# Row stages of a two-block network: the first 128 tokens' factor and turn apart, squares behind the rounded parts, the norm's sums and spreading 7 or 8 blocks later

## The reference

```python
def rmsnorm(x, g):
    xf = x.astype(jnp.float32)
    y = xf * lax.rsqrt(jnp.mean(xf * xf, axis=-1, keepdims=True) + EPS) * g.astype(jnp.float32)
    return y.astype(x.dtype)
...
        mixed = jnp.concatenate([rmsnorm(out_a, g_a), rmsnorm(out_b, g_b), rmsnorm(out_c, g_c)], axis=-1)
        x = x + rmsnorm(mixed @ w_out[l], attn_post_norm[l])

        h = rmsnorm(x, ffn_pre_norm[l])
        u = causal_depthwise_conv(h @ w_up[l], conv_w[l], conv_b[l])
        gate, up = jnp.split(u, 2, axis=-1)
        y = (jax.nn.gelu(gate, approximate=True) * up) @ w_down[l]
        x = x + rmsnorm(y, ffn_post_norm[l])
...
        h = modulate(rms_norm(x, norm_gains[layer, 0]), shift_m, scale_m)
        j = layer // 2
        if layer % 2 == 0:
            y = attn_hybrid_mixer(h, att_w_qkv[j], att_w_o[j], pos)
```

## Time and profile before

| what | value |
|---|---|
| median of 3 runs | 1041.67 us (1041.29 to 1041.73) |
| the profiled execution | 1041.22 us, its span 1039.4 us |
| TensorE matmul busy | 1020.3 us, 98% of the span |
| VectorE busy | 812.4 us, 78% |
| ScalarE busy | 594.4 us, 57% |
| GpSimd busy | 162.5 us, 16% |

### The profile page before, as it was taken

The page is one execution under the profiler, slowest core; times in us unless marked ns, Lnnn a source line. Parts: engine busy times, 40 slices in busy tenths (PEclk is TensorE's granted clock), DMA queues, the critical chain, the costliest instruction groups (busy, mean ns, idle before and its releaser), DMA issues.

```text
span 1039.4 us, 18373 instructions
## 1 busy us (share of the span) xinstructions
PE 1020.3 (98%) x7424; PEld 953.2 (92%) x7424; DVE 812.4 (78%) x1397; ACT 594.4 (57%) x1029; POOL 162.5 (16%) x167
## 2 busy tenths in 40 slices
PE   8999999999999999999999999999999999999997
PEld 8888898999889997999999889988999899999887
DVE  5778799999997977588999798885668676674553
ACT  6688676666446766665444455544465566544443
POOL 0000134333102100032212011201100123111010
PEclk9999999999999999999999999999999999999999
DMA  9833356777893433457998787553434536774441
GB/s 359 312 117 123 122 196 245 289 277 255 344 398 144 154 128 117 193 191 271 381 370 308 282 319 279 203 182 142 162 123 170 195 131 234 278 270 152 168 167 41
DMA packets 34609, 228.49 MB, mean 220 GB/s; under 512 B 3803, under 2 KB 4075, under 8 KB 10972
## 3 DMA queue, kind: packets, MB, share of 16 engines
q1 hardware_dynamic: 33884, 224.69, 57.8%
q0 software_dynamic: 640, 2.62, 0.6%
HBM read 224.68 MB, written 2.62 MB: 219 GB/s over the span
## 4 chain that ended last, share of the span: by engine, by line
PE 84%; DVE 9%; ACT 3%; DMA 2%; issue 1%; POOL 0%; POOLq 0%; SPq 0%; DVEq 0%; ACTq 0%
PE psum L1523 16%; PE psum L1524 15%; PE psum L1525 15%; PE psum L1567 9%; PE psum L1568 5%; DVE w_lo L2300 3%; PE psum L1592 2%; PE psum L1595 2%; PE psum L1594 2%; PE psum L1964 2%; PE psum L1966 2%; PE psum L1965 2%; DMA raw<-in_w_in 2%; ACT w_hi L825 1%; PE psum L1755 1%; DVE arena L2632 1%
## 5 line engine op out<-in xcount | busy, mean ns | idle before, releaser
L2300 DVE TENSOR_TENSOR w_lo<-raw,w_hi 128x1024 fp32r<-128x1024 f32 (+2 forms) x340 | 387.2, 1160 | 134.9 <-ACT w_hi L825 129.4
L825 ACT ACTIVATE w_hi<-raw 128x1024 fp32r<-128x1024 f32 (+2 forms) x340 | 334.3, 997 | 215.7 <-PE psum L1525 84.6
L1523 PE MATMUL psum<-h_hi,w_hi 128*128 128x256 f32 (+1 forms) x1128 | 319.6, 283 | 5.4 <-DVE w_lo L2300 3.1
L1524 PE MATMUL psum<-h_hi,w_lo 128*128 128x256 f32 (+1 forms) x1128 | 316.7, 281 | 0.0
L1525 PE MATMUL psum<-h_lo,w_hi 128*128 128x256 f32 (+1 forms) x1128 | 316.4, 280 | 0.0
L1523 PEld LDWEIGHTS psum<-h_hi,w_hi 128*128 128x128 f32 x1128 | 212.4, 188 | 8.6 <-DVE w_lo L2300 5.2
L1525 PEld LDWEIGHTS psum<-h_lo,w_hi 128*128 128x128 f32 x1128 | 212.3, 188 | 0.0
L1524 PEld LDWEIGHTS psum<-h_hi,w_lo 128*128 128x128 f32 x1128 | 211.6, 188 | 0.7 <-issue 0.7
L1523 PE MATMUL psum<-hid,w_hi 128*128 128x256 f32 (+1 forms) x532 | 152.8, 287 | 0.5 <-DVE w_lo L2300 0.4
L1525 PE MATMUL psum<-hid,w_hi 128*128 128x256 f32 (+1 forms) x532 | 150.0, 282 | 0.0
L1524 PE MATMUL psum<-hid,w_lo 128*128 128x256 f32 (+1 forms) x532 | 150.0, 282 | 0.0
(11 more groups left out here) (316 smaller groups left out, 1386.9 us busy)
## 6 DMA issues: line engine op xcount, KB each, us to landing
arena<-in_ada SPq DMA_DIRECT2D x48, 1024.0 KB, 6.9
raw<-in_gu SPq DMA_DIRECT2D x44, 1024.0 KB, 6.8
raw<-in_ret_in SPq DMA_DIRECT2D x24, 1024.0 KB, 4.8
raw<-in_up SPq DMA_DIRECT2D x22, 1024.0 KB, 4.8
raw<-in_dn SPq DMA_DIRECT2D x32, 704.0 KB, 4.2
raw<-in_qkv SPq DMA_DIRECT2D x12, 1024.0 KB, 5.0
raw<-in_down SPq DMA_DIRECT2D x11, 1024.0 KB, 8.4
raw<-in_ret_o SPq DMA_DIRECT2D x8, 1024.0 KB, 4.8
```

The source lines that it names most:

```text
L825: nc.scalar.activation(w_hi[chunk % SPLIT_SLOTS][:, a:b], raw[chunk % RAW_SLOTS][:, a:b], ACT.Copy)\
L1523: nc.tensor.matmul(out, w[0], hc, start=start, stop=False, skip_group_check=True)
L1524: nc.tensor.matmul(out, w[1], hc, start=False, stop=False, skip_group_check=True)
L2300: tt(w_lo[s][:, a:b], raw[chunk % RAW_SLOTS][:, a:b], w_hi[s][:, a:b].bitcast(F32), ALU.subtract)\
```

## The change

- The mean, the root and the factor are made for each token group r by itself. The means of group 0 follow the first two pieces (`row_mean`, `row_rstd` on VectorE, `row_roots` on ScalarE). Group 0's diagonal is made by ScalarE (`first_diag`), group 1's by VectorE. The factor is written with other constants (1.5 and -0.5 in place of -3 and -0.5), with the same number of operations.
- TensorE turns the eight tiles of group 0 first and then the eight of group 1. The banks of the turned tiles are laid out anew; VectorE is told after tiles 0, 2, 4, 6 and 7 of group 1 (`TURN_ENDS`), and tile 7 waits for the first addition to x, since it reuses tile 0's bank. The 18 filling matmuls become 14 in stage 0, and 4 between the groups in stage 1.
- `rows_by_gains` squares tile 0 after rounding tile 1, then tile 1 after 2, 2 after 4, 3 after 5, and tiles 4 to 7 after 7.
- The sums stand in front of block 9 of chunk 1 and the spreading in front of block 15.

```diff
             def turned_rows(k):
-            return (tra + att)[k // 2][:, k % 2 * S:k % 2 * S + S]
+            bank, at = ((tra[0], 0), (tra[1], 0), (tra[1], S), (att[0], 0), (att[0], S), (att[1], 0), (att[1], S), (tra[0], S))[k]
+            return bank[:, at:at + S]
+
+        TURN_ENDS = (0, 2, 4, 6, 7)
...
+            def row_roots(stage, r):
+                act.wait_ge(row_ms, 2 * stage + r + 1)
+                nc.scalar.activation(row_stat[:, 6 + r:7 + r], row_stat[:, r:r + 1], ACT.Sqrt).then_inc(row_root, 1)
+
+            def first_diag(stage):
+                act.wait_ge(row_factor, stage + 1)
+                nc.scalar.activation(row_diag_of(0), ident[:, :], ACT.Identity, scale=row_stat[:, 24:25]).then_inc(row_diag, 1)
...
                 for r in range(2):
+                    if r:
+                        row_roots(stage, 0)
                     for n in range(2):
                         if r == 1 and n == 1:
+                            first_diag(stage)
                             act.wait_ge(half_done, 2 * (ph.chunk0 + ph.n))
...
             def rows_by_gains(i):
+                squares = {1: (0,), 2: (1,), 4: (2,), 5: (3,), 7: (4, 5, 6, 7)}
                 for k in range(DT):
...
-                    square(i, k)
+                    for n in squares.get(k, ()):
+                        square(i, n)
...
             def turn_rows(ph, i):
                 stage = ROW_STAGE[i]
-                keep_busy(18, att[1])
...
+                if stage == 0:
+                    keep_busy(14, att[1])
+                else:
+                    pe.wait_ge(row_copied, 2)
+                pe.wait_ge(row_diag, 2 * stage + 1)
+                for k in range(DT):
+                    turn(k, 0)
+                if stage:
+                    keep_busy(4, sco[0])
                 units_done(pe, ph.unit0 + ph.units)
                 if stage == 0:
                     pe.wait_ge(row_y, 2)
...
+                pe.wait_ge(row_diag, 2 * stage + 2)
                 for k in range(DT):
...
+                    if k == DT - 1:
+                        pe.wait_ge(row_x, DT * stage + 1)
+                    ins = turn(k, 1)
+                    if k in TURN_ENDS:
                         ins.then_inc(row_turned, 1)
...
-            swiglu_phase("up", FFNPRE, 1, 8)
+            swiglu_phase("up", FFNPRE, 9, 15)
...
-            deferred_phase("qkv", L0, 1, spread_at=8)
+            deferred_phase("qkv", L0, 9, spread_at=15)
...
+            def row_mean(stage, r):
+                dve.wait_ge(row_sq, 4 * stage + 2 * (r + 1))
+                stt(row_stat[:, r:r + 1], row_stat[:, 28 + r:29 + r], EPS, row_stat[:, 30 + r:31 + r], ALU.add, ALU.add).then_inc(row_ms, 1)
+
+            def row_rstd(stage, r):
+                m, s, a, f = (row_stat[:, at + r:at + r + 1] for at in (0, 12, 18, 24))
+                dve.wait_ge(row_root, 2 * stage + r + 1)
+                link(nc.vector.reciprocal(s, row_stat[:, 6 + r:7 + r]))
+                link(stt(a, s, -0.5, m, ALU.mult, ALU.mult))
+                link(tt(a, a, s, ALU.mult))
+                ins = stt(f, a, 1.5, s, ALU.add, ALU.mult)
...
             def row_copies(ph, i):
                 for r, n in ((0, 0), (0, 1), (1, 0)):
+                    if r:
+                        row_mean(ROW_STAGE[i], 0)
+                        row_rstd(ROW_STAGE[i], 0)
...
-                dve.wait_ge(row_sq, 4 * (stage + 1))
-                stt(row_stat[:, 0:2], row_stat[:, 28:30], EPS, row_stat[:, 30:32], ALU.add, ALU.add).then_inc(row_ms, 1)
-                refine(row_root, stage + 1, row_stat, 2)
-                for r in range(2):
-                    ts(row_diag_of(r), ident[:, :], row_stat[:, 24 + r:25 + r], -0.5, ALU.mult, ALU.mult).then_inc(row_diag, 1)
+                if stage == 0:
+                    row_rstd(0, 0)
+                row_mean(stage, 1)
+                row_rstd(stage, 1)
+                ts(row_diag_of(1), ident[:, :], row_stat[:, 25:26], 1.0, ALU.mult, ALU.mult).then_inc(row_diag, 1)
...
             def add_rows(c, first, r, g):
                 for n in range(2):
+                    if (c, r, n) == (3, 1, 1):
+                        row_mean(0, 0)
```

More of the change, by code:

```diff
@@ L367, in build @@
             "rows_done", "row_sq", "row_copied", "row_ms", "row_root", "row_diag", "row_turned", "row_x"))
+        row_factor = sem("row_factor")
         settled_conv, settled_qk = sem("settled_conv"), sem("settled_qk")
@@ L1068, in mix_squares @@
                                              scale=D ** -0.5, accum_out=row_stat[:, at:at + 1]).then_inc(row_sq, 1)
-                act.wait_ge(row_ms, 1)
-                nc.scalar.activation(row_stat[:, 6:8], row_stat[:, 0:2], ACT.Sqrt).then_inc(row_root, 1)
+                first_diag(0)
+                row_roots(0, 1)
             def row_squares(ph, i):
@@ L1083, in row_squares @@
                                              scale=D ** -0.5, accum_out=row_stat[:, at:at + 1]).then_inc(row_sq, 1)
-                act.wait_ge(row_ms, stage + 1)
-                nc.scalar.activation(row_stat[:, 6:8], row_stat[:, 0:2], ACT.Sqrt).then_inc(row_root, 1)
+                row_roots(stage, 1)
                 leave(nc.scalar.activation(row_of(1, 1), row_bank(ph, 1, 1)[:, :], ACT.Copy), ph.unit0 + 1)
             def rows_by_gains(i):
+                squares = {1: (0,), 2: (1,), 4: (2,), 5: (3,), 7: (4, 5, 6, 7)}
                 for k in range(DT):
@@ L1974, in turn_rows, with turn @@
                 stage = ROW_STAGE[i]
-                keep_busy(18, att[1])
+                rows = mix_rows if stage == 0 else e0["y"]
+                def turn(k, r):
+                    return nc.tensor.matmul(turned_rows(k)[:, r * P:(r + 1) * P], rows[:, r * D + k * P:r * D + (k + 1) * P],
+                                            row_diag_of(r), start=True, stop=True)
+                if stage == 0:
[7 more added lines that the diff above has]
+                    keep_busy(4, sco[0])
                 units_done(pe, ph.unit0 + ph.units)
@@ L2363, in norm_h @@
                 tiles_of(i)
+            def row_mean(stage, r):
[8 more added lines that the diff above has]
+                ins = stt(f, a, 1.5, s, ALU.add, ALU.mult)
+                if r == 0:
+                    ins.then_inc(row_factor, 1)
+                else:
+                    link(ins)
             def row_copies(ph, i):
                 for r, n in ((0, 0), (0, 1), (1, 0)):
+                    if r:
+                        row_mean(ROW_STAGE[i], 0)
+                        row_rstd(ROW_STAGE[i], 0)
                     dve.wait_ge(row_sq, 4 * ROW_STAGE[i] + 2 * r + n + 1)
@@ L2391, in row_residual @@
                 for k in range(DT):
-                    if k % 2 == 0:
-                        dve.wait_ge(row_turned, DT // 2 * stage + k // 2 + 1)
+                    if k == 0 or k - 1 in TURN_ENDS:
+                        dve.wait_ge(row_turned, len(TURN_ENDS) * stage + (k + 3) // 2)
                     cut = slice(k * S, (k + 1) * S)
```

10 lines of the change are left out of this document (1 added, 9 removed).

## The result

The changed kernel takes 1048.56 us (median of 6 runs, 1046.59 to 1049.52) beside 1041.48 us of the kernel before (6 runs, 1037.16 to 1041.73): slower by 7.1 us. The ratio on record is 1.0077, with a 95% interval from 1.0062 to 1.0092; the two medians alone divide to 1.0068. The forecast was 1045.8 us, slower, with a range up to 1048.0. The direction was right, the time lies 2.8 us above the figure and 0.6 us above the range.

The account below looks back on a forecast made before the run. Behind the sums, VectorE's chain with ScalarE and GpSimd sets the end, though TensorE is 98% busy overall. Losses of 2.25 us (stage 0) and 1.9 (stage 1), together 4.15, gave 1045.8 us; overall range 1041.6 to 1048.0.

Parts of the forecast that it names:

- The main term: Both row stages: sums eight blocks later in chunk 1, 0.36 us a block, delay VectorE's factor by 2.9 us each.
- marks: Timeline signs: VectorE idle near 2.3 us, chunk 3 pauses 2.5 to 3, turns' wait 0.4 or less, wait at 171.28 arriving 173.5.
- The spreading's cover: Chunk 1 to the scaling: chunk 2's two halves, 2.35 us on VectorE, hide the later spreading, so it costs nothing.
- the gains ahead of chunk 1: Four parts before chunk 1, subtracted from the 2.9 us: 0.65 us in stage 0, 1.0 us in stage 1.
- part 4: GpSimd's last three additions beside chunk 1's low halves: costs 0.15 us per stage, at worst 0.87.
- Parts 1 to 3: Gains: earlier additions to x (0.15 us stage 0, 0.5 stage 1), faster z tiles (0.25), last low part unhindered (0.4).
- The clock falls in the longer pause: Rival: after a 3 us TensorE pause the clock drops to 1.2 GHz, costing 2 to 4 us: 1048 to 1050; chance 0.04.
- A part given back: Rival: behind 150 us something in the chain does not move, so a stage pays less: 1043 us, 1041.7 to 1044.7; chance 0.11.
- Faster by the early start: Rival: chunk 2's and 3's low halves made during VectorE's wait, so stages keep their gains: 1038.7 to 1040.0 us; chance 0.12.

Follow-up runs that it names:

- e3_sums_late_only: Kernel before with only the sums and the spreading moved to blocks 9 and 15 of chunk 1: 1048.13 us beside 1040.82 for before.
- e6_sums_mid: Kernel before with the split turn, squares at once, sums in front of block 5 and spreading in front of block 12: 1044.53 us beside 1041.14.
- e9_turn_and_late: Changed kernel with the squares of x at once again, leaving the split turn and late sums: 1049.73 us beside 1041.25 for before.
- e4_fill_pause: Changed kernel with 16 (up) and 14 (qkv) filling matmuls in chunk 3's pause: 1044.42 us, 3.6 us above before.
- e1_sums_back: Changed kernel with the sums back in front of block 1 and the spreading in front of block 8: 1045.57 us beside 1040.82 for before.
- e5_squares_only: Kernel before with only the squares of x trailing the rounding: 1049.01 us beside 1041.14 for before.
- e8_five_adds: Kernel before with split turn, sums ahead of chunk 1's first block, and five GpSimd additions instead of six in the two stages: 1040.70 us.

## Why the prediction was right in direction and short in size

**The main term was right.** Eight blocks at 0.36 us, 2.9 us in each stage, paid by TensorE in the pause of chunk 3: e3_sums_late_only gives 2.85 us in stage 0, and in stage 1 (351.42 - 321.79) - 26.77 = 2.86 up to the pause. e6_sums_mid gives the half of it for half of the blocks. Most marks were also met: VectorE idle 2.68 us ahead of the factor (2.3 forecast); pauses of 2.31 and 2.21 us in chunk 3, below the 2.5 to 3 forecast, since 0.37 and 0.66 us of the waiting fell ahead of its first block; the turns' wait 0.26 and 0.32 us (0.4 or less). TensorE's wait at 171.28 came at 174.49, with a start 0.48 us later, thus 2.73 us late and not 2.2.

**The spreading's cover held.** Its cost was put at nothing; in the trace of the changed kernel VectorE begins the scaling of stage 0 at 140.82 with no idle time ahead of it.

**Two steps failed.** The stages lost 2.4 us more than the 4.15 of the sum: 1.4 for the clock, which the sum put at nothing, and 1.0 for the gains ahead of chunk 1, most of it part 4.

**The failed step among the gains is part 4**, the other side of 2 and 3: "I take 0.15 us". Parts 1 to 3, forecast at 0.8 us for stage 0 and 1.15 for stage 1, gave 0.66 and 1.00: x's first addition came 0.14 us earlier in stage 0 (123.78 - 119.29, before 123.44 - 118.81), and chunk 1's low halves began 130.82 - 119.29 = 11.53 us after the fillers against 131.00 - 118.81 = 12.19, and in stage 1 331.13 - 320.60 = 10.53 us after the product against 328.94 - 317.41 = 11.53. Then the pair took 1.09 us longer, and TensorE waited 0.56 us for it in each stage. Chunk 1 started only 13.46 - 13.34 = 0.12 us earlier in stage 0 (0.65 forecast) and (330.20 - 317.41) - (332.95 - 320.60) = 0.44 us in stage 1 (1.0 forecast). So part 4 cost 0.54 and 0.56 us in place of 0.15 each. With the main term this gives 2.9 - 0.12 = 2.8 and 2.9 - 0.44 = 2.5 us, measured 2.73 and 2.40: 1.0 us more than forecast, 0.8 of it part 4 and the rest parts 1 to 3. That the trailing squares' gain and this cost cancel is shown by e9_turn_and_late, where both are gone and chunk 1 starts within 0.04 us of the same place. I had the row that priced it, the whole additions of 0.87 us, and took the price of the short operations of z, 0.1 us for each.

The section "SBUF: two separate sides" of the Trainium skill's page "SBUF — State Buffer" lets whichever of the two engines starts first keep the shared ports for its whole instruction. The trace agrees with its direction, not with the prediction's estimate from it: that was 0.87 us at most, one addition, and the pair lost 1.09 us, 0.56 of it seen by TensorE.

**The larger failed step is the clock, at nothing in the sum and at 0.04 among the rivals.** "The clock falls in the longer pause" was treated as another case than the forecast, where it is the same case plus a consequence of it. It fell behind both pauses. Its price of 2 to 4 us was too high, since in stage 0 TensorE has slack behind the pause, as e4_fill_pause shows (2.79 and 2.73 us with and without the full clock): it costs 1.5 us, all in stage 1. That the time came out inside this rival's 1048 to 1050 is in part luck, for 1.0 us of it are the gains'. The chance rested on a wrong reading, too: "it reads full in all slices" can't rule a fall out, since a slice is 26 us and a 9 there means 90% or more. The trace of the kernel before has one, at its start, behind a wait of 1.24 us (the row, then the window with a clock of 0.54):

```profile
9.29 1.82 PE L1664 MATMUL psum<-ident,arena 128*128 128x128 f32 x8 [1.24 <-ACT arena L879]
...
11.00:13.00 2.00, 2.00 (x11) 1.89 (x11) 2.00 (x5) 1.62 (x4) 0.00 (x0) 0.54 0.98 395
```

The section "What's actually happening" of the Trainium skill's page "TensorE: Matmul & The Clock Gate" has the clock halve after idleness, and so speaks for this rival. The windows of the changed kernel agree in direction, 0.50 behind each pause; how long a pause has to be they do not show.

**The account.** 4.15 us forecast; 1.0 from parts 1 to 4, mostly part 4; 1.4 from the clock: 6.5 us, as the stages show. The last 0.6 us to the difference of the medians is within its interval and not assigned.

**The other rivals.** A part given back: no. Between the stages the traces of both kernels are equal within 0.02 us, and the 1.6 us by which the changed kernel's is shorter behind stage 1 go with no part of the change, as said under the table. Faster by the early start: no, VectorE's order kept chunk 2's halves behind the factor, as the argument against it said.

## What to carry to other kernels

Where a reduction's result feeds a serial chain on another engine that has no slack, as here, its place in TensorE's order is paid block by block (8 blocks 2.85 us, 4 blocks 1.44); look whether the input is there earlier, as here, where the sums could stand ahead of the chunk. If work is put off on one engine, look at what it will lie beside at its new place, and price the collision by the longest operation there, not by the shortest. And a growing pause of TensorE can have a second price behind it, the lower clock, which here counted in stage 1, where TensorE itself sets the end, and was nothing in stage 0, where another engine does. Read the clock in windows of 2 us, not from the page's slices.

## What the runs showed of the hardware

- **The clock fell behind single pauses of TensorE shorter than I had thought, and the length of the pause alone does not decide.** In the two stages it fell behind each pause of 2.31, 2.21 and 1.91 us. At 1.7 us it went both ways: behind 1.74 us (e1_sums_back and e6_sums_mid, stage 0) and 1.73 us (e5_squares_only, stage 1) it stayed at 1.00, behind 1.72 us (e1_sums_back, stage 1; e5_squares_only, stage 0) it fell to 0.50. Ahead of the stages, at 41 us, it went both ways with longer ones: 2.16 us in the kernel before and 2.46 in e8_five_adds without a fall, 2.48 in e9_turn_and_late and 1.72 in e3_sums_late_only with one. What decides between them no run here shows. Before and e9_turn_and_late:

```profile
40.56 0.92 PE L1755 MATMUL psum<-arena 64*128 64x256 f32 x8 [2.16 <-ACT arena L950]
...
42.00:44.00 2.00, 2.00 (x13) 2.00 (x12) 1.97 (x8) 0.06 (x1) 0.00 (x0) 1.00 0.00 0
...
41.49 1.27 PE L1771 MATMUL psum<-arena 64*128 64x256 f32 x8 [2.48 <-ACT arena L954]
...
42.00:44.00 2.00, 2.00 (x10) 1.75 (x8) 1.88 (x3) 0.82 (x2) 0.00 (x0) 0.50 0.01 4
```

- **VectorE and GpSimd hold each other up, in these traces more with the wide operation.** A low part of z (128 x 256) took 0.49 us beside GpSimd and 0.39 without it, thus 0.1 us more. A pair of low halves (128 x 1024) took 3.44 us beside three additions of GpSimd and 2.35 us alone, and the three additions took 4.08 us, where the six beside z's narrow operations took 5.23: 1.36 us each against 0.87.
